# Dense feed-forward of an encoder trunk: tokens or weights as the stationary operand

## The reference

```
def swiglu(h, wg, wu, wd):
    return (jax.nn.silu(h @ wg) * (h @ wu)) @ wd
...
        h = rms_norm(x, ffn_pre_g[i])
        j = i // 2
        if i % 2 == 0:
            f = swiglu(h, ffn_w_gate[j], ffn_w_up[j], ffn_w_down[j])
        else:
            f = moe_swiglu(h, router_w[j], router_b[j], moe_w_gate[j], moe_w_up[j], moe_w_down[j])
        x = x + rms_norm(f, ffn_post_g[i])
```

## Time and profile before

| | |
|---|---|
| median of 3 runs | 2094.65 us (2091.22 to 2096.89) |
| profiled execution, first to last instruction | 2090.3 us |
| PE, DVE, ACT busy | 96%, 71%, 53% |
| dense stage, first to last product | 353.7 to 627.7 us |
| mixers of layer 0 / of layer 1 | to 343 us / 669 to about 1020 us |
| expert stage | about 1020 to 2035 us |
| mean DMA rate over the span / in the dense stage | 242 / 178 GB/s |

### The profile page before, as it was taken

One profiled execution on the slowest core, in us unless ns is written; L12 is line 12 of the kernel. 1 busy time (PEld: TensorE's weight loads), 2 busy tenths in 40 slices (PEclk: granted clock), 3 DMA queues, 4 the chain that ended last, 5 costly groups with the idle time before them and its releaser, 6 DMA issues.

```text
span 2090.3 us, 26963 instructions
## 1 busy us (share of the span) xinstructions
PE 2006.6 (96%) x9934; PEld 1679.5 (80%) x9934; DVE 1482.1 (71%) x1632; ACT 1097.9 (53%) x1128; POOL 57.3 (3%) x104
## 2 busy tenths in 40 slices
PE   6999998999998999999799999999999999999986
PEld 5888787999996878888688888888888888888864
DVE  3358676555546427868588988888888888988864
ACT  4232324333325332223477777777777777777743
POOL 2100002000002100000000000000000000000000
PEclk9999999999999999999799999999999999999998
DMA  8533335555535533323599999999989999999970
GB/s 296 161 101 101 101 102 184 183 181 184 189 132 215 187 109 113 101 87 115 206 336 345 350 369 344 355 342 353 366 326 371 345 357 347 352 372 332 365 290 29
DMA packets 253343, 506.67 MB, mean 242 GB/s; under 512 B 8304, under 2 KB 90384, under 8 KB 253152
## 3 DMA queue, kind: packets, MB, share of 16 engines
q1 hardware_dynamic: 250592, 497.92, 67.1%
q0 software_dynamic: 2688, 7.91, 1.3%
HBM read 504.75 MB, written 1.05 MB: 242 GB/s over the span
## 4 chain that ended last, share of the span: by engine, by line
PE 83%; DVE 8%; ACT 3%; issue 3%; DMA 2%; POOL 0%; SPq 0%; DVEq 0%; ACTq 0%; POOLq 0%
PE ps L1022 26%; PE ps L964 18%; PE ps L934 9%; PE ps L1168 7%; PE ps L866 4%; PE ps L1109 4%; PE ps L844 3%; PE ps L1152 2%; PE ps L1175 2%; DVE egate L1982 2%; PE ps L909 2%; DMA ring<-in_moe_w_down_dram 2%; PE ps L974 1%; PE ps L983 1%; ACT down_hi_w L1371 1%
## 5 line engine op out<-in xcount | busy, mean ns | idle before, releaser
L1802 DVE TENSOR_TENSOR ring_lo<-ring,up_gate_hi_w 128x2048 fp32r<-128x2048 f32 x224 | 505.2, 2288 | 66.6 <-ACT up_gate_hi_w L1368 65.0
L1368 ACT CAST up_gate_hi_w<-ring 128x2048 fp32r<-128x2048 f32 x224 | 423.7, 1914 | 91.3 <-DMA ring<-in_moe_w_up_dram 87.1
L1022 PE MATMUL ps<-up_gate_hi_w,tokens_hi 128*128 128x512 f32 x896 | 355.9, 397 | 1.5 <-DVE ring_lo L1802 1.5
L1022 PE MATMUL ps<-up_gate_hi_w,tokens_lo 128*128 128x512 f32 x896 | 350.2, 391 | 0.0
L1022 PE MATMUL ps<-ring_lo,tokens_hi 128*128 128x512 f32 x896 | 349.4, 390 | 0.0
L1807 DVE TENSOR_TENSOR down_lo_w<-ring,down_hi_w 128x2048 fp32r<-128x2048 f32 x112 | 256.5, 2290 | 50.2 <-ACT down_hi_w L1371 50.0
L1168 PE MATMUL ps<-hT,ring 128*128 128x256 f32 x1024 | 232.2, 380 | 0.6 <-DVE xn L1988 0.6
L1371 ACT CAST down_hi_w<-ring 128x2048 fp32r<-128x2048 f32 x112 | 214.0, 1911 | 25.7 <-DMA ring<-in_moe_w_down_dram 25.6
L1168 PEld LDWEIGHTS ps<-hT,ring 128*128 128x128 f32 x1024 | 193.1, 190 | 28.2 <-DVE xn L1988 1.8
L1022 PEld LDWEIGHTS ps<-up_gate_hi_w,tokens_lo 128*128 128x128 f32 x896 | 168.5, 188 | 36.1
L1022 PEld LDWEIGHTS ps<-up_gate_hi_w,tokens_hi 128*128 128x128 f32 x896 | 168.7, 188 | 35.6 <-issue 1.9
(11 more groups left out here) (221 smaller groups left out, 2712.5 us busy)
## 6 DMA issues: line engine op xcount, KB each, us to landing
ring<-in_moe_w_up_dram SPq DMA_DIRECT2D x112, 1024.0 KB, 5.1
ring<-in_moe_w_gate_dram SPq DMA_DIRECT2D x112, 1024.0 KB, 5.2
ring<-in_moe_w_down_dram SPq DMA_DIRECT2D x112, 1024.0 KB, 8.5
ring<-in_w_in_dram SPq DMA_DIRECT2D x58, 1024.0 KB, 5.4
ring<-in_ffn_w_up_dram SPq DMA_DIRECT2D x16, 1024.0 KB, 5.5
ring<-in_ffn_w_gate_dram SPq DMA_DIRECT2D x16, 1024.0 KB, 8.0
ring<-in_ffn_w_down_dram SPq DMA_DIRECT2D x16, 1024.0 KB, 9.8
ring<-in_w_branch_dram SPq DMA_DIRECT2D x8, 1024.0 KB, 5.1
```

The costliest lines, as they stand in the source:

```text
L1022: m = mm(bank, xs[:, 4 * half + k, :], w[:, k, :], start=(half == k == n == 0), stop=(half == 1 and k == 3 and n == 2))
L1368: copy(up_gate_hi_w[:, j, :], ring[:, slot, :]).then_inc(run.up_gate_hi, 1)
L1802: v.tensor_tensor(ring_lo[:, slot, :], ring[:, slot, :], up_gate_hi_w[:, j, :], ALU.subtract)\
```

## The change

The dense stage takes the expert stage's form. Chunks of 512 hidden features (`FF_CHUNKS` = 8): slots 0 and 1 hold the two halves of the width (`k` 0 to 3, 4 to 7) of 512 gate columns, 2 and 3 those of up, 4 and 5 two halves of down. `ffn_half` multiplies one slot by one token tile: tokens stationary, 512 weight columns moving, 12 matmuls. Gate fills banks 0 and 1 (one a token tile), up banks 2 and 3. DVE multiplies silu by up into `hidden`, PE transposes it back into banks 2 and 3 (`ffn_turn`, four transposes a tile), ACT and DVE split it, and the down product is as before. On PE a chunk is: gate half 0 of b, turn of b-1, gate half 1 of b, down of b-1, up of b. Chunk 0 starts with token tile 0 as soon as that one is split. Silu of both tiles, the casts and the subtractions are reordered on ACT and DVE, and SP loads in the order 0, 1, 4, 5, 2, 3 from chunk 1 on. `hidden` and `silu` get 1024 columns each in the work area.

```
+FF_CHUNKS = D_FF // ECW
...
+            def ffn_loads(b):
+                for j in range(RING) if isinstance(b, int) else (0, 1, 4, 5, 2, 3):
+                    if isinstance(b, int):
+                        sp.wait_ge(*released(LOOPS[0] - RING + j))
+                    elif j < 4:
+                        sp.wait_ge(ffn.up_gate_used, 4 * (b - 1) + j + 1)
+                    else:
+                        sp.wait_ge(ffn.down_split, 2 * (b - 1) + j - 3)
+                    dst = ring[:, ring_slot(j), :].rearrange("p (k c) -> p k c", k=4 if j < 4 else 2)
+                    sp.dma_start(dst, ffn_views[j // 2][b][j % 2]).then_inc(slot_in[ring_slot(j)], 16)
...
+            def ffn_half(b, j, t):
+                half = j % 2
...
+                for k in range(4):
+                    for n, (xs, w) in enumerate(((hT_hi, hi), (hT_hi, lo), (hT_lo, hi))):
+                        m = mm(ps[:, 2 * (j // 2) + t, :], xs[:, 4 * half + k, t * P:(t + 1) * P], w[:, k, :],
+                               start=(half == k == n == 0), stop=(half == 1 and k == 3 and n == 2))
+            def ffn_gate_first():
+                for t in range(NT):
+                    pe.wait_ge(tile_split, tile_number(0, "fpre", t, 1) + 1)
+                    for j in (0, 1):
+                        pe.wait_ge(ffn.up_gate_split, j + 1)
+                        m = ffn_half(0, j, t)
+                        if t == 1 and j == 0:
+                            m.then_inc(ffn.up_gate_used, 1)
...
+            def ffn_gate(b, j):
+                pe.wait_ge(ffn.up_gate_split, 4 * b + j + 1)
+                for t in range(NT):
+                    if j == 0:
+                        pe.wait_ge(ffn.silu_ready, NT * (b - 1) + t + 1)
...
+            def ffn_up(b):
+                for j in (2, 3):
+                    pe.wait_ge(ffn.up_gate_split, 4 * b + j + 1)
+                    for t in range(NT):
+                        if j == 2:
+                            wait_from(pe, ffn.turned_split, NT * (b - 1) + t + 1)
+                        m = ffn_half(b, j, t)
+                        if j == 3 and t == 0:
+                            m.then_inc(ffn.up_ready, 1)
+                    m.then_inc(ffn.up_gate_used, 1)
+            def ffn_turn(b):
+                for t in range(NT):
+                    pe.wait_ge(ffn.hidden_ready, NT * b + t + 1)
+                    for j in range(E_BLOCKS):
+                        m = nc.tensor.transpose(ps[:, 2 + t, j * P:(j + 1) * P], hidden[:, t, j * P:(j + 1) * P], ident)
+                    m.then_inc(ffn.turned, 1)
+            def ffn_down(b, first=False, last=False):
+                for j in range(E_BLOCKS):
+                    if j % 2 == 0:
+                        pe.wait_ge(ffn.down_split, 2 * b + j // 2 + 1)
+                    for t in range(NT):
+                        if j == 0:
+                            pe.wait_ge(ffn.turned_split, NT * b + t + 1)
+                        m = down_product(acc, (t,), j, first and j == 0, last and j == E_BLOCKS - 1)
+                    if j % 2:
+                        m.then_inc(ffn.down_done, 1)
+            def feed_forward():
+                ffn_gate_first()
+                ffn_up(0)
+                ffn_gate(1, 0)
+                ffn_turn(0)
+                ffn_gate(1, 1)
+                ffn_down(0, first=True)
+                ffn_up(1)
+                with pe.Fori(2, FF_CHUNKS) as b:
+                    ffn_gate(b, 0)
+                    ffn_turn(b - 1)
+                    ffn_gate(b, 1)
+                    ffn_down(b - 1)
+                    ffn_up(b)
+                ffn_turn(FF_CHUNKS - 1)
+                ffn_down(FF_CHUNKS - 1, last=True)
...
+            # ACT
+            def ffn_chunk(b, first=False, last=False):
+                ffn_his(b, 2)
+                if not first:
+                    for t in range(NT):
+                        ffn_turned_hi(b - 1, t)
+                ffn_his(b, 3)
+                ffn_silu(b, 0)
+                if not last:
+                    ffn_his(b + 1, 0)
+                ffn_silu(b, 1)
+                ffn_his(b, 4)
+                if not last:
+                    ffn_his(b + 1, 1)
+                ffn_his(b, 5)
...
+            # DVE
+            def ffn_chunk(b, first=False, last=False):
+                if not first:
+                    for t in range(NT):
+                        ffn_hidden(b - 1, t)
+                ffn_los(b, 2)
+                if not first:
+                    for t in range(NT):
+                        ffn_turned_lo(b - 1, t)
+                ffn_los(b, 3)
+                if not last:
+                    ffn_los(b + 1, 0)
+                ffn_los(b, 4)
+                if not last:
+                    ffn_los(b + 1, 1)
+                ffn_los(b, 5)
```

More of the change, by code:

```diff
@@ L705, in _ @@
                     ffn_loads(0)
[L706 to L707 removed]
+                    with sp.Fori(1, FF_CHUNKS) as b:
+                        ffn_loads(b)
                 else:
@@ L1201, in _ @@
                 if layer % 2 == 0:
-                    pe.wait_ge(tile_split, tile_number(layer, "fpre", NT - 1, 1) + 1)
-                    feed_forward(0)
-                    with pe.Fori(1, FF_BODIES) as body:
-                        feed_forward(body, more="go on")
-                    feed_forward(FF_BODIES, more="end")
+                    feed_forward()
                 else:
@@ L1537, in _ @@
                 if layer % 2 == 0:
-                    silus(0)
-                    with act.Fori(1, FF_BODIES - 1) as body:
-                        silus(body)
-                    silus(FF_BODIES - 1, last=True)
-                    act.wait_ge(ffn.down_done, N_FFN_BLOCKS)
+                    ffn_chunk(0, first=True)
+                    ffn_chunk(1)
+                    with act.Fori(2, FF_CHUNKS - 1) as b:
+                        ffn_chunk(b)
+                    ffn_chunk(FF_CHUNKS - 1, last=True)
+                    for t in range(NT):
+                        ffn_turned_hi(FF_CHUNKS - 1, t)
+                    act.wait_ge(ffn.down_done, 2 * FF_CHUNKS)
                     for t in range(NT):
@@ L2008, in _ @@
                     tile_los(layer, "fpre", 1)
-                    hiddens(0)
-                    with dve.Fori(1, FF_BODIES - 1) as body:
-                        hiddens(body)
-                    hiddens(FF_BODIES - 1, last=True)
-                    dve.wait_ge(ffn.down_done, N_FFN_BLOCKS)
+                    ffn_chunk(0, first=True)
+                    ffn_chunk(1)
+                    with dve.Fori(2, FF_CHUNKS - 1) as b:
+                        ffn_chunk(b)
+                    ffn_chunk(FF_CHUNKS - 1, last=True)
+                    for t in range(NT):
+                        ffn_hidden(FF_CHUNKS - 1, t)
+                    for t in range(NT):
+                        ffn_turned_lo(FF_CHUNKS - 1, t)
+                    dve.wait_ge(ffn.down_done, 2 * FF_CHUNKS)
                     for t in range(NT):
```

185 lines of the change are left out of this document (74 added, 111 removed).

## The result

The changed kernel takes 2097.29 us (median), the kernel before 2092.31 beside it: ratio 1.0021, 95% interval 1.0015 to 1.0028 (20 executions of each). It is slower, and by less than the 0.3% from which the prediction counts a difference. The profiled executions, one of each kernel, last 2094.1 and 2090.3 us.

What follows compares the result with a forecast made beforehand. TensorE's (PE's) pitch was taken to bound the dense stage. Chunks -2.9, head -0.7, first gap +5.1, clock after it +2.0 and tail +1.2 gave +4.7 on 2094.65: 2099.4 us, range 2091 to 2108.

Steps and rivals of the forecast that it cites:

- chunks: Dense stage's eight chunks on PE: wide products save more than transposes add, 269.1 against 272.0 us, gain 2.9 (1.4 to 3.7).
- head: Start of the dense stage: first product 1.6 us earlier, 0.9 more lost at half clock, net -0.7 us.
- first turn waits: PE's first transposing back of hidden, ahead of the first down product: no wait was forecast, 0 us.
- first gap: Ahead of the first down product: PE idle 5.1 us (2.6 to 8.1), as chunk 1's up half 0 load goes out late.
- clock after it: First products behind the idle stretch before the first down product run at half clock: 2.0 us lost (1.5 to 2.5).
- tail: End of the dense stage: last turn and down have no product between them, 2.1 us less the transposes' 0.88, +1.2 us.
- sum of the stage: All terms of the dense stage added: +4.7 us, bounds -1.4 to about +16.
- behind the stage: Step after the dense stage: its weight loads are freed earlier, but it waits for PE alone, so nothing is gained.
- Steady cover: Later chunks: ACT's 13.8 and DVE's 16.5 us fit in 33.6, slack 3.2 us before the down product, no stall.
- the walk: Step-by-step timing of loads, casts and subtractions in a steady chunk: turned subtractions end at 8.6, needed at 11.8, slack 3.2 us.
- g: Moment when PE has done gate half 0 of chunk 0 for both token tiles; first-chunk times are counted from it.
- the expert stage's cold end: Rival at the stage's end: gaps around the last transposes exceed 3 us and the clock falls; +10.7, 2105.4 us, chance 0.14.

Runs made afterwards that it cites:

- experiment 6b: Changed kernel with 704 of the 768 wide gate and up products split into two of 256 columns; ratio 1.0066 to the kernel before.
- 6a: Changed kernel with every transpose of hidden in the dense stage issued twice, 128 instead of 64; ratio 1.0060 to the kernel before.
- Experiment 5a: Changed kernel with POOL's loads of the next layer's parameters held back until the second down product; ratio 1.0035 to the kernel before.
- experiment 5: Two kernels: the changed one with POOL's next-layer parameter loads held back, to the second down product or the last chunk; ratios 1.0035 and 1.0007 to the kernel before.
- experiments 1: Changed kernel with only SP's load order in chunk 1 edited, up before down; ratio 0.9997 to the kernel before.
- experiment 2: Changed kernel with ACT's down casts and DVE's down subtractions of chunk 0 moved before the work on chunk 1's gate 0; ratio 0.9984 to the kernel before.
- experiment 3: Changed kernel with both SP's new load order in chunk 1 and ACT's and DVE's new order in chunk 0; ratio 0.9987 to the kernel before.
- Experiment 4b: Changed kernel with 32 products of unused result put before the first down product; ratio 1.0014 to the kernel before.
- experiment 4a: Changed kernel with 22 products of unused result put before the first down product; ratio 1.0022 to the kernel before.
- 5b: Changed kernel with POOL's loads of the next layer's parameters held back until the last chunk; ratio 1.0007 to the kernel before.
- experiment 7: Changed kernel with the first gate products waiting for both token tiles, as before the change; ratio 1.0030 to the kernel before.

## Why the forecast was right, step by step

The measured 2097.29 us lies in the range of 2091 to 2108, and 0.21% is "the same" by the prediction's 0.3%. The forecast of 2099.4 stood on a median of three, 2094.65; twenty executions of the kernel before gave 2092.31, from which +4.7 leads to 2097.0. The mechanism was right. That the sum of the stage is met within 0.3 us is partly luck: chunks and head came out 2.0 us better than forecast, the first turn, the gap and the clock 2.2 us worse.

| step | forecast | measured |
|---|---|---|
| chunks | -2.9 | 8 x (33.55 - 34.0) = -3.6 |
| head | -0.7 | -2.0 |
| first turn waits | 0 | +1.1 |
| first gap | +5.1 | +5.5 |
| clock after it | +2.0 | +2.7 |
| tail | +1.2 | 2.09 - 0.88 = +1.2 |
| sum of the stage | +4.7 | +4.9 (seen 4.96) |
| behind the stage | 0 | not the change's, as far as is known (below) |

**Chunks: right.** The period came to the sum without the expert stage's edge, 144 x 0.2269 + 0.88 = 33.55. The 0.013 us for two narrow against one wide product is shown by experiment 6b, and the 0.88 by 6a. The Trainium skill, TensorE: Matmul & The Clock Gate, section Back-to-back issue gap, gives the isolated gap as columns / 2.4 + 2.5 ns. Splitting a product would by that cost 2.5 ns (an estimate from that page); the run gives 13.

**Steady cover: right.** No wait in chunks 2 to 7 of the changed kernel. Experiment 5a measures the slack: a landing 7.1 us later than forecast (15.0 against 7.9) costs 2.8, so 4.3 us; the walk gave 3.2, 4.1 if only the first turned subtraction counts, for which PE waits first.

**First gap: right in mechanism; that its size is met is luck.** Let g be 362.2, the moment that the prediction calls g. Gate 0 landed 2.7 us later than forecast (8.1 instead of 5.4), up 0 0.9 earlier (7.0 instead of 7.9): the chain ends at g + 32.2 instead of 30.5. PE came to ask later too, 26.8 instead of 25.4, 1.1 of it by the first turn's wait, so the gap stays 5.3 (5.5 in the table, counted from start to start). What I failed to see is the row of POOL's loads in the opening: I took gate 0's landing from a load that had the DMA engines to itself. With POOL's loads away the gap is 3.7 (experiment 5). The cause, the orders in which SP and in which ACT and DVE take their work, is shown from two sides (1 and 2).

**Head: half right.** The start was 1.75 us earlier, forecast 1.6. The clock term was wrong: I let the clock rise when it had before. It rose 4.5 us after the opening transposes instead of 7.5, and the slow stretch cost no more than before (1.4 against 1.7). In other kernels with the same opening products it cost 0.7 (experiment 2) to 1.9 (experiment 3), so the size of this term is in part chance. Part of what the head won went into the first turn's wait, +1.1, which I had at nothing, since by my landing of gate 0 the four subtractions ended in time.

**Clock after the gap: right in kind,** low by 0.7: 14 slow products, 5.85 us against 3.18. Experiment 4b shows that the idle time causes it.

**Tail: right.** The rival, the expert stage's cold end, failed: 0.40 and 0.44 us idle and no slow product.

**Behind the stage: not refuted.** I wrote that nothing is gained there. The 1.7 us that the float32 products are shorter show in some kernels that have the change and not in others, so they aren't shown to be its gain. From 2090.3 to 2094.1, 3.8 us, the profiled executions differ by these parts: opening 0.7 later, stage +5.0, float32 products -1.7, expert stage -2.2, what follows it +1.7, the rest +0.4. All but the stage lie in code that isn't edited. The medians differ by 5.0 (3.1 to 5.9 by the interval), forecast 4.7.

## What to carry to other kernels

Count a change's start-up and its end by themselves: here eight chunks brought 3.6 us and the first one took 9. Walk each engine's program once for the first iteration, writing down when each load goes out, when its slot was free, and what stands ahead of it; the fix here was one other order for one chunk, SP's alone or ACT's and DVE's. Measure an edit in its own stage too: here unedited stages differed by up to 6.6 us between kernels. And look at which other queues load in that stretch before taking a landing time from elsewhere.

## What I had not expected of the hardware

- The clock fell behind 1.83 us idle (experiment 4a), though it was kept behind 1.69, in the same stage behind 1.00, and ahead of the float32 products behind 2.39 in eight of thirteen profiled executions. So the length of the idle stretch alone doesn't decide. In the changed kernel the granted clock fell 1.3 us before PE resumed; in 5a, behind 3.73 us idle, 1.2 us after it: five warm products from 391.15, then slow ones.
- Where the granted clock rises after the opening transposes varies from 2.9 us (experiment 2) through 4.5 (changed) and 5.7 (experiment 3) to 8.4 (experiment 7), with the same products in the first three.
- The eight plain float32 products behind the stage take 8.8 or 7.1 us; the difference is slow clock (before: their records stand 0.855 us apart up to 633.8, then half of that). What decides is open: of experiments 1 and 5b, whose stages end at 626.8 and 628.1, the first shows the longer, the second the shorter.
- The 1 MB load of gate 0 takes 5.1 to 5.3 us without POOL's loads beside it (experiment 5), 7.5 to 9.5 beside them in the nine kernels that issue it as the changed one does, and that of up 0 15.0 beside some of them in 5a.
- At the low clock a product of 256 columns stands 0.213 us from the next and one of 512 columns 0.427: exactly twice. The narrow one's extra 7 ns is there at full clock alone.
